# Two layers in fp32 on one core: seven channel groups of one projection computed by seven products of half-sized blocks instead of eight

## What is computed

```python
h = rmsnorm(x, norm_g)
proj = jnp.einsum('bld,dn->bln', h, w_in)
v, bg, cg, za, u, zb, ga, gb = jnp.split(proj, SPLITS, axis=-1)
ya = bg * causal_depthwise_conv(cg * v, conv_w)
ya = jnp.einsum('blc,cd->bld', ya * jax.nn.silu(za), w_out_a)
yb = jax.nn.gelu(s5_scan(u, a_re, a_im, log_dt, b_re, b_im, c_re, c_im, d_skip))
...
```

## Time and profile before

| | us |
|---|---|
| median of 3 runs | 2513.88 (2513.25 to 2514.46) |
| the profiled execution | 2516.84 |
| its span, first to last instruction | 2515.6 |
| PE busy in it | 2496.6 (99%) |
| DVE / ACT / POOL busy | 1592.1 (63%) / 857.1 (34%) / 369.9 (15%) |
| DMA, all queues | 353.08 MB, mean 140 GB/s |

### The profile page before, as it was taken

How to read it: one execution, slowest core, us unless ns; L and a number is a source line. 1 busy time by engine, 2 the same in 40 slices (tenths; PEclk the granted TensorE clock), 3 DMA queues, 4 the chain that set the end, 5 groups by cost and what they waited for, 6 DMA issues and landing times.

```text
span 2515.6 us, 30050 instructions
## 1 busy us (share of the span) xinstructions
PE 2496.6 (99%) x11932; PEld 2158.8 (86%) x11932; DVE 1592.1 (63%) x2161; ACT 857.1 (34%) x1171; POOL 369.9 (15%) x286
## 2 busy tenths in 40 slices
PE   9899999999999999999999999999999999999998
PEld 8788888888888888888888888878888888888888
DVE  7976666668777777743756666557566564467534
ACT  5322222222222222223432223333465664324432
POOL 2133343334333343100000000000000000000001
PEclk9999999999999999999999999999999999999999
DMA  5243433333333333333576667524322222556333
GB/s 195 90 147 132 138 136 129 135 121 124 98 126 115 114 116 110 108 105 109 188 253 228 226 233 235 184 90 154 106 84 84 85 77 91 190 169 209 126 126 126
DMA packets 117964, 353.08 MB, mean 140 GB/s; under 512 B 15424, under 2 KB 18752, under 8 KB 117824
## 3 DMA queue, kind: packets, MB, share of 16 engines
q1 hardware_dynamic: 117824, 351.16, 41.5%
HBM read 321.68 MB, written 23.07 MB: 137 GB/s over the span
## 4 chain that ended last, share of the span: by engine, by line
PE 96%; DVE 2%; DMA 1%; ACT 0%; SPq 0%; issue 0%; DVEq 0%; ACTq 0%
PE bank L561 28%; PE bank L563 28%; PE bank L562 28%; PE bank L764 2%; PE bank L765 2%; PE bank L763 2%; PE bank L817 1%; PE bank L807 1%; PE bank L624 1%; PE bank L727 1%; PE bank L612 1%; DMA W<-in_w 1%; DVE WL L1307 0%; DVE SM L1394 0%; PE bank L800 0%; PE bank L798 0%
## 5 line engine op out<-in xcount | busy, mean ns | idle before, releaser
L1307 DVE TENSOR_TENSOR WL<-W,WH 128x1024 fp32r<-128x1024 f32 (+1 forms) x452 | 585.9, 1298 | 563.4 <-ACT WH L936 561.8
L936 ACT ACTIVATE WH<-W 128x1024 fp32r<-128x1024 f32 (+1 forms) x452 | 473.8, 1050 | 953.6 <-PE bank L563 671.7
L561 PE MATMUL bank<-hH,WH 128*128 128x512 f32 x1792 | 682.6, 381 | 8.6 <-DVE hL L1636 5.7
L563 PE MATMUL bank<-hH,WL 128*128 128x512 f32 x1792 | 680.5, 380 | 0.0
L562 PE MATMUL bank<-hL,WH 128*128 128x512 f32 x1792 | 680.4, 380 | 0.0
L561 PEld LDWEIGHTS bank<-hH,WH 128*128 128x128 f32 x1792 | 339.5, 189 | 67.8 <-issue 13.1
L563 PEld LDWEIGHTS bank<-hH,WL 128*128 128x128 f32 x1792 | 339.4, 189 | 48.4
L562 PEld LDWEIGHTS bank<-hL,WH 128*128 128x128 f32 x1792 | 339.6, 190 | 47.5
L561 PE MATMUL bank<-h2H,WH 128*128 128x512 f32 x624 | 239.6, 384 | 0.1
L562 PE MATMUL bank<-h2L,WH 128*128 128x512 f32 x624 | 236.5, 379 | 0.0
L563 PE MATMUL bank<-h2H,WL 128*128 128x512 f32 x624 | 236.5, 379 | 0.0
(11 more groups left out here) (306 smaller groups left out, 3534.2 us busy)
## 6 DMA issues: line engine op xcount, KB each, us to landing
W<-in_w SPq DMA_DIRECT2D x332, 512.0 KB, 3.6
W<-in_ada SPq DMA_DIRECT2D x96, 512.0 KB, 4.1
W<-in_wa SPq DMA_DIRECT2D x32, 512.0 KB, 4.2
W<-in_wo SPq DMA_DIRECT2D x32, 512.0 KB, 3.7
W<-in_wvv SPq DMA_DIRECT2D x32, 512.0 KB, 4.1
W<-in_wb SPq DMA_DIRECT2D x16, 512.0 KB, 4.5
URAW<-U SPq DMA_DIRECT2D x96, 64.0 KB, 3.1
scr_ga<-SO SPq DMA_DIRECT2D x16, 256.0 KB, 2.0
```

The lines of the kernel that those rows point to most:

```text
L561: e.matmul(o, wh, xh, start=first, stop=False)
L563: return e.matmul(o, wl, xh, start=False, stop=last)
L936: e.activation(chunk_parts(n)[0][:, c], W[:, i % NW, c], ACT.Copy).then_inc(sem["hi"], 1)
L1307: e.tensor_tensor(wl[:, c], W[:, plan.item_of[n] % NW, c], wh[:, c].bitcast(F32), ALU.subtract).then_inc(sem["lo_v"], 1)
```

## The change

**Seven products.** Channel groups 9 to 15 are taken in 14 units each. The tokens are cut in halves (256 each), the input channels in halves (`kc`), the output channels in pairs of parts (v with cg: j = 1 or 0 by `ST_PARTS`, bg with za). Each pair is a product of 2x2 blocks, done by seven block products instead of eight; the two pairs j take turns. A unit is now 24 matmuls of 256 columns (`strassen_product`). Product f takes as weights B11, B21, B11+B12, B22, B11+B12+B22, B22+B12 and the sum of all four (signs lie in the factors), and as input a half of `hH`/`hL` or one of four sums of halves (S1 to S3, and S4, which is written over a half of `hH`/`hL`).

**Weight sums.** Six of the 14 chunks (products 0, 1, 3) are plain loads by SP. The other eight are DMAs on POOL's queue that add the next raw chunk to what lies in the slot (`accum_op`). Each waits for the `lo` of the unit four places before, which read the slot last. There are six slots: three of `W` and three new (`WX`).

**Output.** Partial sums are read out of PSUM between products: ACT copies six of them a group (256 columns, to `SI`), DVE adds six corners (`corner_11`, `corner_12`, `corner_22`). PE's units 12 and 13 wait for the corners of units 10 and 11. Convolution and gating follow at units 10 to 13 and at the next group's unit 0.

**Input sums.** In group 8, which is computed as before, DVE and ACT make S1 to S4 (`factor_sums`, `factor_high`, `last_factor_low`): 22 instructions of 1024 elements a row on DVE, 8 on ACT.

**Other moves.** The state-space tiles end with group 7 (`SSM_C` = 7). Gelu goes to group 10. The multiplication of `XS` by `RSA` goes from POOL to DVE (`scaled_rows`, units 10 to 15). The last two projections of u, and the first two of zb, run in pairs: both first halves, then both second halves. `normed` goes four rows at a time, ahead of the units 16 to 19.

```diff
+SSM_C = 7
+ST_C = 9
+ST_PARTS = ((2, 0), (1, 3))
+ST_SLOTS = (0, 0, 1, 1, 0, 0, 2, 2, 0, 0, 2, 2, 0, 0)
...
+        self.two_rows("u", [[w1[64 + m, c] for c in range(2)] for m in range(2)])
+        for m in range(2, 6):
+            self.proj("u", [w1[64 + m, c] for c in range(2)])
+        self.two_rows("u", [[w1[64 + m, c] for c in range(2)] for m in (6, 7)])
+        self.two_rows("zb", [[w1[72 + m, c] for c in range(2)] for m in range(2)])
...
+        for c in range(ST_C):
...
+        self.strassen_units(w1)
...
+        for c in range(ST_C, 16):
...
+            for i in range(14):
+                n, j = n0 + i, i % 2
+                s = slots[ST_SLOTS[i]][j]
...
+                (b11, b12), (b21, b22) = b[j]
+                raw, added = ((b11, None), (b21, None), (None, b12), (b22, None), (None, b22), (None, b12),
+                              (None, b21))[i // 2]
+                if raw is not None:
...
+                    self.base[c, i] = (s, raw, user.get(s))
...
+                    self.sums[c, i] = (s, added, user[s])
...
+                user[s] = ("unit", n)
+            slots = slots[1:] + slots[:1]
...
+        return bank[(0, 1, 2, 4, 5, 6)[r + 3 * j] if r or c % 2 == ST_C % 2 else (3, 7)[j]]
...
+        def base(c, i):
...
+            s, src, user = plan.base[c, i]
+            if user is not None:
+                e.wait_ge(*slot_free(user))
+            elif s > NW:
+                e.wait_ge(*nth("st_l", 0))
+            e.dma_start(raw_chunk(plan.strassen[c] + i), src).then_inc(w_base[s], 16)
...
+        for i in (0, 1, 2, 3, 6, 7):
+            base(ST_C, i)
...
+        for c in range(ST_C, 16):
+            if c < 15:
+                base(c + 1, 0)
+                base(c + 1, 1)
...
+            if c < 15:
+                for i in (2, 3, 6, 7):
+                    base(c + 1, i)
...
+        def project_two(ps, XH, XL, ready=None, beside=None):
...
+            for kc in range(2):
+                for p in ps:
+                    n = unit()
+                    if beside is not None:
+                        beside(n)
+                    products(n, p, kc, 0, 15, XH, XL, ready if p == ps[0] else None)
...
-        for p in u_p[2:]:
+        for p in u_p[2:6]:
             project(p, xh, xl, beside=norm)
+        project_two(u_p[6:], xh, xl, beside=ssm_until)
...
+        project_two(spill_p[:2], xh, xl, n_ready, beside=ssm_until)
+        for p in spill_p[2:] + a_p:
+            project(p, xh, xl, beside=ssm_until)
...
+        factors = [(first_half(hH, 0), first_half(hL, 0)), (first_half(hH, 8), first_half(hL, 8)),
+                   (whole(S1H), whole(S1L)), (second_half(hH, 0), second_half(hL, 0)),
+                   (whole(S2H), whole(S2L)), (whole(S3H), whole(S3L)), (second_half(hH, 8), second_half(hL, 8))]
...
+        def strassen_product(c, i):
+
+            f, j, g = i // 2, i % 2, c - ST_C
+            n = unit()
+            r = (0, 1, 2, 2, 0, 0, 0)[f]
...
+            elif f == 3:
+                e.wait_ge(*nth("st_a", g, 3 + j))
...
+            elif f == 4:
+                e.wait_ge(*nth("st_a", g, 1 + j))
+            elif f == 5:
+                e.wait_ge(*nth("st_a", g, 5 + j))
+            else:
+                e.wait_ge(*nth("st_v", g, (5, 7)[j]))
+            xh_, xl_ = factors[f]
+            o = r_bank(c, r, j)[:, 0:256]
+            for k8 in range(8):
...
+                e.matmul(o, wh, x_h, start=begins, stop=False, skip_group_check=True)
+                e.matmul(o, wh, x_l, start=False, stop=False, skip_group_check=True)
+                mm = e.matmul(o, wl, x_h, start=False, stop=ends, skip_group_check=True)
+            mm.then_inc(sem["used"], 1)
...
-            e.wait_ge(sem["used"], plan.last(u_p[7]) + k // 8)
+            e.wait_ge(sem["used"], plan.units(u_p[7])[k // 8] + 1)
...
+        for i in range(4):
+            for k in range(4 * i, 4 * i + 4):
+                normed(k)
+            ssm_until(unit())
...
+        def factor_high(batch):
...
+            for f, (o, x) in enumerate(((S1H, SX[2]), (S3H, SX[1]), (S2H, SX[0]))):
+                e.wait_ge(*nth("st_x", 0, 8 * batch + (5, 6, 7)[f]))
+                e.activation(o[:, 4 * batch:4 * batch + 4, :], x[:, :, :], ACT.Copy).then_inc(sem["st_h"], 1)
...
+                        for batch in range(2):
+                            e.wait_ge(*nth("st_x", 0, 8 * batch + 8))
+                            e.activation(hH[:, 4 * batch:4 * batch + 4, half[1]], SX4[batch][:, :, :],
+                                         ACT.Copy).then_inc(sem["s4_h"], 1)
...
+        def strassen_gate(c):
+            e.wait_ge(*nth("st_v", c - ST_C, 7))
+            x = T[:, 2, :]
+            e.activation(x, x, ACT.Silu, scale=-1.0).then_inc(sem["st_a"], 1)
...
+            g = c - ST_C
+            for i in range(14):
+                if i in (1, 2, 5, 6, 9, 10):
...
+                    unit_done(c, i - 1)
...
+                    e.activation(MC[m], r_bank(c, 2 if 4 < i < 8 else 0, j)[:, 0:256],
+                                 ACT.Copy).then_inc(sem["st_a"], 1)
+                unit()
...
+                if i == 12:
+                    strassen_gate(c)
...
+        def scaled_rows(ks):
+            for k in ks:
+                e.wait_ge(*nth("xsq", k))
+                e.wait_ge(*nth("xl", k))
+                e.tensor_tensor(XS[:, k, :], XS[:, k, :], RSA[:, :], ALU.mult).then_inc(sem["xn"], 1)
...
+                for i in range(2):
                     keep_u(i)
+            if m == 5:
+                keep_u(4)
+                scaled_rows(range(4))
             ssm_until(unit())
             if m == 3:
                 inv_rms(0, 3, 0, 0)
-            else:
...
+            if m == 4:
+                keep_u(2)
+                keep_u(3)
+            if m == 5:
+                scaled_rows(range(4, 8))
+        for i in range(4):
+            ssm_until(unit())
+            if i == 0:
+                keep_u(5)
+            scaled_rows(range(8 + 2 * i, 10 + 2 * i))
...
-        for k in range(8):
-            normed(k)
-        for s in range(len(spill_p)):
+        for i in range(4):
+            for k in range(4 * i, 4 * i + 4):
+                normed(k)
...
+            if i == 1:
+                keep_u(6)
+                keep_u(7)
...
+            for x, ks, h in ((a, k, 0), (b, k, 1), (d, l, 1), (s4, l, 0)):
+                e.tensor_tensor(x, f32(hH[:, ks, half[h]]), f32(hL[:, ks, half[h]]),
+                                ALU.add).then_inc(sem["st_x"], 1)
+            yield
+            e.wait_ge(*nth("st_x", 0, 8 * batch + 3))
+            e.tensor_tensor(d, d, b, ALU.subtract).then_inc(sem["st_x"], 1)
...
+            e.scalar_tensor_tensor(out=a, in0=d, scalar=-1.0, in1=a, op0=ALU.mult,
+                                   op1=ALU.subtract).then_inc(sem["st_x"], 1)
+            e.wait_ge(*nth("st_x", 0, 8 * batch + 7))
+            e.scalar_tensor_tensor(out=s4, in0=s4, scalar=-1.0, in1=a, op0=ALU.mult,
...
+            for f, (lo_, hi_, x) in enumerate(((S1L, S1H, d), (S3L, S3H, b), (S2L, S2H, a))):
+                e.wait_ge(*nth("st_h", 0, 3 * batch + f + 1))
+                e.tensor_tensor(lo_[:, k, :], x, f32(hi_[:, k, :]), ALU.subtract).then_inc(sem["st_l"], 1)
...
+        def corner_22(c, j):
+
...
+            a, b = MC[2 + j], r_bank(c, 0, j)[:, 0:256]
+            e.tensor_tensor(o_, a if j == 0 else tokens(a), b if j == 0 else tokens(b),
+                            ALU.add).then_inc(sem["st_v"], 1)
...
+                corner_12(c, 0)
...
+                e.tensor_tensor(halves(cv[:, half[0]]), tokens(x11[0]), tokens(x12[0]),
+                                ALU.mult).then_inc(sem["st_v"], 1)
+            if i == 11:
+                corner_22(c, 0)
+                corner_12(c, 1)
+            if i == 12:
+                corner_22(c, 1)
+            if i == 13:
+                unit_done(c, 12)
...
+                e.tensor_tensor(halves(cv[:, half[1]]), tokens(r_bank(c, 0, 0)[:, 0:256]), tokens(x22[0]),
+                                ALU.mult).then_inc(sem["st_v"], 1)
...
+                e.tensor_scalar(o, CV[:, 0:512], taps[0], None, ALU.mult).then_inc(sem["st_v"], 1)
...
+                    e.scalar_tensor_tensor(out=o, in0=CV[:, x:512 + x], scalar=taps[x], in1=o, op0=ALU.mult,
+                                           op1=ALU.add).then_inc(sem["st_v"], 1)
...
+                e.scalar_tensor_tensor(out=halves(x), in0=halves(x), scalar=-1.0, in1=tokens(x11[1]),
+                                       op0=ALU.mult, op1=ALU.mult).then_inc(sem["st_v"], 1)
...
+                e.scalar_tensor_tensor(out=halves(x), in0=halves(x), scalar=-1.0,
+                                       in1=tokens(r_bank(c, 0, 1)[:, 0:256]), op0=ALU.mult,
+                                       op1=ALU.mult).then_inc(sem["st_v"], 1)
...
+                e.tensor_tensor(SO[:, c % 2, :], o, T[:, 2, :], ALU.mult).then_inc(sem["st_v"], 1)
...
+        for c in range(ST_C, 16):
```

(51 more changed lines are left out.)

271 lines of the change are left out of this document (211 added, 60 removed).

## The result

| | before | the change |
|---|---|---|
| median of 4 runs | 2514.17 (2513.25 to 2516.80) | 2502.69 (2502.57 to 2502.88) |
| ratio, 95% interval | 1 | 0.9953 (0.9935 to 0.9970) |
| the profiled execution, its span | 2516.84, 2515.6 | 2502.73, 2501.5 |

The change is faster by 11.5 us by the medians (7.5 to 16.3 by the interval). The forecast was 20.2 us and a time of 2493.7. From span to span it is 14.1 us: the profiled execution of before is the highest of its four, 2.7 us above their median. These four lie low: in the later runs the kernel before had medians of 2515.40 to 2516.43.

The account below looks back on a forecast made before the run. The prediction took PE's back-to-back matmuls as the bound, with 12.2 us in holes and slow clock. Its terms, -27.3 + 3.0 + 2.4 + 0.7 + 0.5 + 0.5 + 0, gave -20.2 us: 2493.7 us, range 2478 to 2514.

Parts of the forecast that it names:

- term 1: PE's matmuls in the seven groups: 336 of 256 columns replace 192 of 512, 3.90 us less a group, -27.3 us.
- term 2: End of stage u: the old hole and its slow clock go, but `normed` comes late on DVE; +3 us, between -3 and +6.
- The walk: DVE's queue at the end of u, followed by instruction durations: PE holes of 4.7, 2.8, 2.8 and 3.9 us.
- Term 3: Waits inside seven-product groups: unit 12 late by 0.34 us for `corner_22`, +2.4 us; +0.7 for a bank in the first group.
- Term 4: DVE ahead of the seven groups: denser state-space tiles and group 8's input sums may delay `lo`; +0.5 us each.
- Term 5: DMAs in the seven groups: throughput and landing time of the adding transfers cost PE 0, bounds 0 and +10 us.
- limit (a): DMA throughput in a group: additions at x times a plain chunk's engine time fill the group at x = 2.2.
- Limit (b): Latency of additions chained in one slot: 8.4 us free per link, 9.3 with the spare time before `lo`'s use.
- Rival 3: End of stage u: `normed` starts in time, holes and slow clock vanish; -12.2 instead of +3, 2478.5 us; chance 0.12.
- Rivals 1 and 2: Seven groups: adding DMAs bind from x = 2.5 (2561 us at x = 3), or land after 9.3 us (2504); chance 0.13 each.
- rival 4: Groups 0 to 8: DVE's backlog reaches PE, with holes and slow stretches in tight places; +8, 2502 us; chance 0.08.

Follow-up runs that it names:

- e5_oldu: The changed kernel with the old end of stage u put back (projections unpaired, `normed` eight rows at a time, `XS` by `RSA` on POOL): 2492.44 us, before beside it 2516.34.
- e1_keep: The changed kernel with `keep_u` 6 and 7 moved ahead of the `lo` of unit 19: 2495.12 us, before beside it 2516.34.
- e3_corner: The changed kernel with both `corner_22` additions issued ahead of their unit's `lo`: 2499.58 us, before beside it 2516.43.
- e8_eight: The changed kernel with eight groups by seven products instead of seven, tiles ending a group earlier: 2498.35 us, before beside it 2515.40.
- e7_five: The changed kernel with five extra plain 512 KB transfers in each of groups 9 to 14: 2503.15 us, before beside it 2516.43.
- The repeat: The changed kernel run again unaltered, in a later set: 2501.43 us, before beside it 2516.43.
- e9_best: e1_keep and e3_corner together, with state-space parameter instructions held from unit 15 and gently caught up: 2480.61 us, before beside it 2515.40.
- e4_plain: The changed kernel with its adding DMAs made plain loads, weight sums not formed: 2501.71 us, before beside it 2516.43.

## Why the prediction came out as it did

The measured 2502.69 us lies inside the range (2478 to 2514), and the mechanisms of most terms were right. But one term came out at more than three times its size, and the reference was a high execution.

- **Bound, term 1.** Right. Matmuls of 256 columns start 111.7 ns apart in the groups too: -27.3 us. PE's busy time fell by 22.8 and not by 27, mostly since the slow matmuls of term 2 count as busy (3.9 us more than before).
- **Term 2, the end of u.** This step failed: +3 forecast, +9.7 in the trace, +8.9 by e5_oldu. Its own parts, 14.2 + 1.7 against 12.2 before, already gave 3.7. The first half was right: with `XS` by `RSA` on DVE, the hole at 75.67 went, and DVE's six small instructions take 1.32 us. The walk gave four holes of 4.7, 2.8, 2.8 and 3.9 us, 14.2 in all. There came three of 4.7, 6.7 and 3.4, 14.8 in all: the sum agreed by luck. The walk followed only what `normed` waits for. It left out that the pairing moves the second zb projection from unit 18 to 17, while `keep_u` for its bank moves behind the `lo` of 19. In turn the slow clock hid the hole before row 4, and the wait on U hid that before row 8; with U out of the way all four show (e1_keep). And the slow clock was sized wrongly: I allowed one stretch (1.7 us), while it fell behind each of the three holes, 6.9 us. That alone is 5.2 of the 6.7 us in this profile. It isn't a fixed price: the six other profiles with this end of u have 4.3 to 6.7 us, with holes of 14.8 to 15.9.
- **Term 3.** Mechanism right, e3_corner confirms it. The size is 0.48 us a group instead of 0.34, 3.4 instead of 2.4 us: the wait itself is 0.39, as PE starts 0.15 us behind the addition's end where I had put 0.12 without a row, and the next distances are 0.09 us longer as well. The 0.7 us at the first group didn't come.
- **Term 4.** +1.0 forecast, 0 measured: PE never waits on `WL` ahead of the seven groups. DVE's 87% (forecast 90) stayed within the lead of its `lo`; e8_eight shows that even 96% does.
- **Term 5.** 0, right, and the additions landed in 5.8 us, far below 9.3. An addition took 2.95 us of the engines against 1.56 for a plain chunk. The Trainium skill (Collectives: The Full Stack, Terms) gives a reducing transfer two source reads and about half the rate of a copy; the measured factor of 1.9 agrees. What the Trainium skill warns of (SBUF — State Buffer, the trap "DVE blocks DMA"), POOL kept from writing descriptors, is shown by no run here: POOL's plain loads landed in 3.8 to 4.3 us, SP's in 3.3 to 3.5. My limit (a) of x = 2.2, from the share, was too strict: e7_five ran at a share of 1.00 with nearly no loss. Limit (b) fits all three: 5.8, 7.8 and 10.1 us.
- **The total.** From profile to profile: -0.5 at the start, +9.7, -27.3, +3.4, and +0.4 behind the groups make -14.3, with the 0.25 us longer step to the next stage -14.1 (spans: -14.1). By the medians it is -11.5, since the sum was taken from a profiled execution 2.7 us above its median. The repeat gave -15.0. So of the 8.7 us missed, 6.7 are term 2, 2.7 the reference, and the rest nearly cancels: +1.0 of term 3, -0.7 and -1.0 that didn't come, -0.5 and the two small steps.
- **Rivals.** None of the four is what happened. Rival 3 (the place is cured) was possible with two more moves: e9_best. Rivals 1 and 2 are out by e4_plain, and rival 4 didn't show.

## What to carry to other kernels

When a step is moved ahead of its old place, list for each buffer or bank it needs who frees it, and what that reader now stands behind; a reader behind a `lo` whose `hi` waits for PE makes PE wait for itself. When a hole is priced, price the slow clock behind it too, as a range: here nothing to 3 us a hole. A weight sum by an adding DMA cost PE nothing here, and about twice a plain transfer in engine time; watch how long it takes to land against what its chain allows, and not the share alone.
